# Per-head sums of squares: four tiles at a time in four column groups of TensorE, in place of one call for each tile

## The chip, the cores and the metric

The kernel runs on one core of one Trainium2 chip. The metric is the device time of one execution in microseconds. Three executions of the kernel before took 913.89, 914.31 and 915.83 us; the median, 914.31 us, is what the changed kernel is compared with.

## What is computed

Two transformer blocks over 512 tokens of width 1024, in f32. The first has gated mixing, a forgetting attention and a convolved feed-forward layer. The second, in which the change lies, has four heads of a gated delta rule (heads of 128) and four heads of a differential attention (each with two halves of 64). The parts that matter:

```python
# delta rule: q and k from a causal convolution with silu, heads of 128
q = l2norm(q) * 128 ** -0.5         # x * rsqrt(sum(x * x) + EPS)
k = l2norm(k)
# differential attention: 4 heads, 2 halves of 64 each
q = rmsnorm(q.reshape(b, t, 4, 2, 64), q_gain) * 64 ** -0.5
k = rmsnorm(k.reshape(b, t, 4, 2, 64), k_gain)
s = einsum('bqhcd,bkhcd->bhcqk', q, k)       # causal softmax over k
wts = p[:, :, 0] - lam * p[:, :, 1]
```

Each norm needs, for each token and head (or half head), a sum of squares over the head's channels.

## The kernel before

Activations are kept with channels on the partitions and tokens along the free dimension: a tile is 128 channels x 512 tokens. Large products are made in three f32r passes (a high and a low half of each operand, `three`, line 662), one weight tile of 128 x 1024 ("unit") at a time, from a ring of four slots that SP and POOL fill by DMA and whose low halves VectorE (DVE) makes (`ring_low`).

The second block follows one list, MIX2_ORDER (lines 339 to 353), that all engines walk in the same order. Each engine acts on the items that concern it, strictly in that order, and semaphores tie them together. The stages, in order:

- `_projections`: `kqv` 0 to 11 are the products of the delta rule's k (0 to 3), q (4 to 7) and v (8 to 11). `taps` is the convolution on DVE, then a silu on ScalarE (ACT) and, for q, a square into SQ2. The k norms come from elsewhere (the diagonal of the Gram matrices). `l2s` (line 1144, `head_sums` 924) sums the squares of one q tile: `token_sums` (723) makes four matmuls, in each of which 128 tokens of the squares are the stationary operand and a column of ones moves, so that the sums come out with tokens on the partitions. `l2r` (2093) copies them to L2C.
- `_diff_values`: `dfv` is the product of the attention's values, into banks 0, 6, 7, 1; between its parts run the decays, the Gram products and the start of the inverse.
- QUERIES_KEYS (line 143): `dfqk` (n, part) is an eighth of the product of tile n, q and k by turns. Tile n - 1 is squared by ACT at part 0 (1485) and summed at part 5 (`qk_sums`, 932), the last one at item (8, 1), with two moving columns for the two halves of a head, into bank 6. `qr` (1486) takes the root on ACT and the reciprocal on DVE (2105) for four tiles. `rs` or `kn` (1490) spreads a key's factors over RS on ACT; `kn` transposes RS into bank 7 (`spread_key`, 938) and DVE multiplies the key tile by it (2025). These items are mixed by `_prepare` and `_spread` (103, 262) with the steps of two block inverses (Y, Z, X, W), as their fills.
- `_attention(4)` (176) makes slots 0 to 18. Slot n holds D of n - 1, A of n and B of n - 2, and in every fourth from 6 on C. A: scores on PE (`df_scores`, 1076), masked maximum on DVE (`masked_max`, 2029), exponentials on ACT (1538). D: the difference of the two weightings, on DVE (2039). B: transposes on PE (`df_turn`, 1088) and a copy to PT2 on ACT (1548), which the next B on PE waits for. C: `df_attend` (1098). Between them stand eighths of the last projection, `z`. `_last_norms` (116) puts the last sums, `qr` 1, `rs` 2, `kn` 2, `rs` 3 and `kn` 3 into the first slots.

The first block has products in two column groups of the array already: `attend` (823) writes partitions 0 to 63 and 64 to 127 of a bank from two heads, with widths of 512, 384, 256 and 128 columns. `rows_to_columns` (917) transposes 128 x 512 in four steps.

## Time and profile before

| what | value |
|---|---|
| median of three runs | 914.31 us (913.89 to 915.83) |
| profiled execution, span from the first to the last instruction | 911.8 us |
| PE, matmuls | 896.3 us busy, 4467 records |
| PE, weight loads | 725.4 us |
| DVE | 556.8 us, 980 instructions |
| ACT | 291.4 us, 594 instructions |
| granted clock of PE over the span | 1.000 |

The page gives no other time of the profiled execution than its span. A busy time is the union of an engine's spans. Matmuls are pipelined: the durations shown overlap, so what a group of matmuls costs is read from starts, not from durations. An f32 matmul appears as two records, each with a weight load of its own; an f32r matmul or a transpose as one. Times in rows are microseconds from the span's start unless marked ns; "idle before <- releaser" is the time an engine stood idle ahead of an instruction and what released it.

### The profile page before, as it was taken

The numbers are of one execution on the slowest core, as the hardware profiler recorded it, in microseconds if no ns is written. First come the engines' busy times: TensorE is split into PE (matmuls) and PEld (weight loads), VectorE is DVE, ScalarE is ACT, GpSimd is POOL, SyncE is SP. The second block draws the span as 40 slices with busy tenths as digits, with TensorE's granted clock in tenths as the row PEclk, the third lists the DMA queues.
The fourth block names the chain that finished last, engine by engine and source line by source line (L and its number), as shares of the span: only waits on it lengthen the run. The fifth ranks groups of instructions, "written<-read, shape, count | busy, mean of one in ns | idle before, by whom it ended". The sixth has DMA issues, their size and how long they took to land.

```text
span 911.8 us, 13208 instructions
## 1 busy us (share of the span) xinstructions
PE 896.3 (98%) x4467; PEld 725.4 (80%) x4467; DVE 556.8 (61%) x980; ACT 291.4 (32%) x594; POOL 72.4 (8%) x138
## 2 busy tenths in 40 slices
PE   9999998999999999999999999999999999999998
PEld 7887766688888888888888888888888897567887
DVE  7248467355877777767743334497787473875555
ACT  6234466524322222222210101353231113444710
POOL 0000000000010110000100000000000000000000
PEclk9999999999999999999999999999999999999999
DMA  8856443254765566655566655568556222221554
GB/s 276 245 192 195 152 139 116 93 162 133 236 203 189 184 193 194 202 193 184 189 195 196 196 192 185 184 211 252 173 151 183 73 92 93 93 82 59 181 174 153
DMA packets 53861, 154.74 MB, mean 170 GB/s; under 512 B 9629, under 2 KB 15021, under 8 KB 53689
## 3 DMA queue, kind: packets, MB, share of 16 engines
q1 hardware_dynamic: 22320, 75.70, 26.0%
q0 software_dynamic: 19008, 69.21, 23.4%
q10 hardware_dynamic: 12488, 9.23, 3.3%
q8 instruction: 29, 0.48, 0.2%
q14 instruction: 16, 0.12, 0.0%
HBM read 149.63 MB, written 4.49 MB: 169 GB/s over the span
## 4 chain that ended last, share of the span: by engine, by line
PE 88%; DVE 5%; issue 3%; DMA 3%; ACT 2%; DVEq 0%; SPq 0%; POOLq 0%; ACTq 0%
PE bank L668 75%; DMA HI<-wstream 2%; PE bank L727 1%; PE bank L1104 1%; PE bank L805 1%; PE bank L1084 1%; DVE LO L1634 1%; PE bank L829 1%; PE bank L1015 1%; PE bank L1001 1%; PE bank L819 1%; PE bank L1095 1%; DMA RAW<-wstream 1%; DVE SQ L1616 0%; PE bank L1037 0%
## 5 line engine op out<-in xcount | busy, mean ns | idle before, releaser
L668 PE MATMUL bank<-GH,HI 128*128 128x512 f32 (+1 forms) x724 | 292.7, 404 | 1.1 <-issue 1.1
L668 PE MATMUL bank<-GH,LO 128*128 128x512 f32 (+1 forms) x724 | 281.8, 389 | 0.0
L668 PE MATMUL bank<-GL,HI 128*128 128x512 f32 (+1 forms) x724 | 281.4, 389 | 0.0
L1634 DVE TENSOR_TENSOR LO<-RAW,HI 128x1024 fp32r<-128x1024 f32 x88 | 107.6, 1223 | 119.3 <-DMA HI<-wstream 118.4
L668 PEld LDWEIGHTS bank<-GH,HI 128*128 128x128 f32 x724 | 136.1, 188 | 35.9 <-issue 9.8
L668 PEld LDWEIGHTS bank<-GH,LO 128*128 128x128 f32 x724 | 135.9, 188 | 28.8
L668 PEld LDWEIGHTS bank<-GL,HI 128*128 128x128 f32 x724 | 136.3, 188 | 23.4
L650 POOL DMA_DIRECT2D HI<-wstream x132 | 69.8, 529 | 815.3 <-PE bank L668 805.4
L1346 ACT ACTIVATE YC<-AB,PAR 128x512 f32<-128x512 f32 x44 | 36.0, 818 | 140.7 <-DVE AB L1798 140.7
L668 PE MATMUL bank<-AH,HI 128*128 128x512 f32 x176 | 69.4, 394 | 0.0
L668 PE MATMUL bank<-AH,LO 128*128 128x512 f32 x176 | 69.0, 392 | 0.0
L668 PE MATMUL bank<-AL,HI 128*128 128x512 f32 x176 | 68.3, 388 | 0.0
L1798 DVE TENSOR_TENSOR AB<-bank,RB 128x512 f32<-128x512 f32 x44 | 30.4, 691 | 48.9 <-PE bank L668 48.8
L1792 DVE TENSOR_TENSOR LO<-RAW,HI 128x1024 fp32r<-128x1024 f32 x44 | 53.6, 1218 | 3.2 <-DMA HI<-wstream 3.2
L668 PEld LDWEIGHTS bank<-AH,LO 128*128 128x128 f32 x176 | 33.0, 188 | 7.7
L1225 ACT ACTIVATE GH<-X,SM 128x512 fp32r<-128x512 f32 x8 | 5.8, 724 | 104.4 <-DVE X L1856 104.4
L668 PEld LDWEIGHTS bank<-AL,HI 128*128 128x128 f32 x176 | 33.0, 188 | 7.4
L668 PE MATMUL bank<-HI,GH 128*128 128x512 f32 x96 | 38.2, 398 | 0.5 <-DVE LO L1641 0.5
L668 PEld LDWEIGHTS bank<-AH,HI 128*128 128x128 f32 x176 | 33.1, 188 | 6.6
L668 PE MATMUL bank<-LO,GH 128*128 128x512 f32 x96 | 37.4, 390 | 0.0
L668 PE MATMUL bank<-HI,GL 128*128 128x512 f32 x96 | 37.4, 389 | 0.0
L1809 DVE SCALAR_TENSOR_TENSOR YC<-AB,PAR,YC 128x512 f32<-128x512 f32 x44 | 33.1, 751 | 6.0 <-DVE YC L1805 0.3
(309 smaller groups left out, 1173.3 us busy)
## 6 DMA issues: line engine op xcount, KB each, us to landing
RAW<-wstream SPq DMA_DIRECT2D x135, 512.0 KB, 3.7
HI<-wstream POOLq DMA_DIRECT2D x132, 512.0 KB, 5.0
X<-x_t SPq DMA_DIRECT2D x8, 256.0 KB, 7.6
NCB<-out_t ACTq DMA_DIRECT2D x8, 256.0 KB, 4.2
out_t<-X ACTq DMA_DIRECT2D x8, 256.0 KB, 5.5
XR<-out_t ACTq DMA_DIRECT2D x8, 256.0 KB, 3.5
out_t<-XR SPq DMA_DIRECT2D x7, 256.0 KB, 3.6
EG<-out_t ACTq DMA_DIRECT2D x1, 1024.0 KB, 6.1
```

Source lines behind the costliest of these rows:

```text
L650: pool.dma_start(HI[:, s, :], wstream[bass.ds(2 * i + s // 2, 1), :, 1024 * (s % 2):1024 * (s % 2 + 1)] .rearrange("o p n -> p (o n)")).th ...
L668: mm = pe.matmul(out, a, b, start=(first and n == 0), stop=(last and n == 2))
L727: mm = pe.matmul(out[:, n * b:n * (b + 1)], src[:, P * b:P * (b + 1)], groups, start=True, stop=True)
L805: mm = pe.matmul(PS[2 + e][:, 0:w], q[r, 4 + p, P * i:P * (i + 1)], k[r, p, 0:w], start=(part == 0), stop=(part == 2))
L819: mm = pe.transpose(PS[4 + e][:, P * j:P * (j + 1)], P1[:, 2 * (n % 2) + e, P * j:P * (j + 1)], IDENT)
L829: mm = pe.matmul(PS[6][64 * e:64 * e + 64, P * j:T], VB[:, j, P * p + 64 * e:P * p + 64 * (e + 1)], PT1[:, e, j, P * j:T], start=(j == 0), ...
L1001: mm = pe.matmul(narrow(A, h, l), NT[:, h, b, :], even(XI[:, h, b, :], l), start=True, stop=True)
L1346: act.activation(YC[:, gv, :], AB[:, gv, 2:T + 2], ACT.Identity, scale=PAR[:, bass.ds(6 * t + (C_FCW + 3 * gv + 2), 1)], bias=PAR[:, bass. ...
L1634: dve.tensor_tensor(LO[:, u % RING, :], RAW[:, u % RING, :], HI[:, u % RING, :].bitcast(F32), ALU.subtract).then_inc(unit_split, 1)
L1792: dve.tensor_tensor(LO[:, slot, :], RAW[:, slot, :], HI[:, slot, :].bitcast(F32), ALU.subtract).then_inc(unit_split, 1)
L1798: dve.tensor_tensor(AB[:, gv, 2:T + 2], up_bank(G_UP + 2 * tt + gv)[:, :], RB[:, :], ALU.mult)\
L1809: dve.scalar_tensor_tensor(YC[:, gv, :], AB[:, gv, 0:T], PAR[:, bass.ds(6 * t + (C_FCW + 3 * gv), 1)], YC[:, gv, :], ALU.mult, ALU.add).th ...
```

## The change

The sums are made for four tiles in one call, `four_sums`. Matmul j has 32 columns as its stationary operand (ones, or the indicators of the two half heads, 16 columns each) and all 512 tokens of tile j's squares as the moving one, and writes partitions 32j to 32j + 31 of bank 7, so that each uses one group of 32 columns of the array. The bank now holds rows with tokens along the free dimension. ACT copies it to SBUF (`l2c`, `qc`), and PE transposes the copy back into bank 7 (`turned_rows`; `l2t`, `qt`), from where `l2r` and `qr` read one column of each 32 or 16. SQ2 and SQD grow from two tiles to four. The items are moved: the sums of the delta rule's q stand behind `kqv` 9, their transposes behind `kqv` 10 and `l2r` behind the taps of tile 10. The first four of the attention's q and k are summed at (4, 5). In attention `qc` 1 stands ahead of A0, `qt` 1 behind A0, `qr` 1 behind A1, `rs` 2 and `kn` 2 in slots 2 and 3, `rs` 3 and `kn` 3 in slot 4. There are new waits: `dfv` waits for `l2r`, C of head 0 for all keys.

```diff
--- before.py
+++ after.py
@@ -115,10 +115,11 @@
 
 def _last_norms(slots):
 
-    slots[0] = [("z", (0, 0)), ("P", 0), QUERIES_KEYS[-1], ("qr", 1), ("rs", 2)] + slots[0]
-    slots[1] += [("P", 1), ("kn", 2)]
-    slots[2].insert(0, ("rs", 3))
-    slots[3] += [("P", 2), ("kn", 3)]
+    slots[0] = [("z", (0, 0)), ("P", 0), QUERIES_KEYS[-1], ("qc", 1)] + slots[0]
+    slots[1] = [("qt", 1)] + slots[1] + [("P", 1), ("qr", 1)]
+    slots[2] += [("rs", 2)]
+    slots[3] += [("P", 2), ("kn", 2)]
+    slots[4] = [("rs", 3)] + slots[4] + [("kn", 3)]
     return slots
 
 
@@ -146,7 +147,11 @@
     for n in range(9):
         for part in range(KC if n < 8 else 2):
             order.append(("dfqk", (n, part)))
-            if (n, part) == (5, 0):
+            if (n, part) == (4, 5):
+                order.append(("qc", 0))
+            elif (n, part) == (4, 7):
+                order.append(("qt", 0))
+            elif (n, part) == (5, 0):
                 order.append(("qr", 0))
             elif (n, part) in ((5, 4), (6, 0)):
                 order.append(("kn", n - 5))
@@ -274,8 +279,8 @@
 
     order = [("ba", 0), ("rows", 0)]
     for t in range(12):
-        if t in (6, 10):
-            order.append(("l2r", t // 4 - 1))
+        if t in (6, 11):
+            order.append(("l2r", t // 8))
         order.append(("kqv", t))
         if t == 0:
             order += [("lam", 0), ("rows", 1)]
@@ -287,8 +292,10 @@
             order.append(("cols", 0))
         if 4 <= t <= 7:
             order.append(("spill", t - 4))
-        if 6 <= t <= 9:
-            order.append(("l2s", t - 2))
+        if t == 9:
+            order += [("l2s", 0), ("l2c", 0)]
+        if t == 10:
+            order.append(("l2t", 0))
         if t == 7:
             order.append(("bt", 0))
         if t == 9:
@@ -340,8 +347,8 @@
     _projections()
     + _diff_values()
     + QUERIES_KEYS[:8] + [("T2", 1)] + QUERIES_KEYS[8:10] + [("scatter", 1)] + QUERIES_KEYS[10:21] + [("X", (0, 3)), ("X", (1, 3))] + QUERIES_KEYS[21:24]
-    + _prepare(0, QUERIES_KEYS[24:43])
-    + _prepare(2, QUERIES_KEYS[43:-1])
+    + _prepare(0, QUERIES_KEYS[24:45])
+    + _prepare(2, QUERIES_KEYS[45:-1])
     + _with_products(_last_norms(_attention(4)), _eighths(range(5))[1:36], [])
     + _merge(_eighths(range(4, 6))[4:13],
              _merge(_scans(range(3)), [("os", t) for t in range(4)] + [("or", 0)] + [("on", t) for t in range(4)]))
@@ -438,7 +445,7 @@
         R1 = place("R1", [P, T], F32, TR + 5 * KB)
         R2 = place("R2", [P, T], F32, TR + 7 * KB)
         BR = place("BR", [P, T], F32, TR + 11 * KB)
-        SQ2 = place("SQ2", [P, 2, T], F32, TR + 13 * KB)
+        SQ2 = place("SQ2", [P, 4, T], F32, TR + 13 * KB)
         ZT = place("ZT", [P, 8, T], F32, TR)
         SQO = place("SQO", [P, 2, T], F32, TR + 16 * KB)
         DQ = place("DQ", [P, 4, T], F32, arena + 72 * KB)
@@ -447,7 +454,7 @@
         RS = place("RS", [P, T], F32, arena + 96 * KB)
         ST = place("ST", [P, 4, P], F32, arena + 98 * KB)
 
-        SQD = place("SQD", [P, 2, T], F32, X_AT)
+        SQD = place("SQD", [P, 4, T], F32, X_AT)
         P0 = place("P0", [P, 3, T], F32, X_AT)
         PB = place("PB", [P, T], F32, X_AT + 6 * KB)
         PT2 = place("PT2", [P, NB, T], F32, X_AT + 8 * KB)
@@ -482,6 +489,7 @@
         IDENT, ONES, HALF = (CON[:, c:c + P] for c in (K_ID, K_ONE, K_HALF))
         CAUSAL = CON[:, K_CAUSAL:K_CAUSAL + 512]
         GNEG = CON[:, K_GNEG:K_GNEG + P]
+        ONES32, HALF32 = CON[:, K_ONE:K_ONE + 32], CON[:, K_HALF + 48:K_HALF + 80]
 
         def level_mask(l):
             n = MASKED.index(l)
@@ -725,6 +733,18 @@
                 n = groups.shape[1]
                 for b in range(NB):
                     mm = pe.matmul(out[:, n * b:n * (b + 1)], src[:, P * b:P * (b + 1)], groups, start=True, stop=True)
+                return mm
+
+            def four_sums(out, tiles, groups):
+
+                for j in range(4):
+                    mm = pe.matmul(out[32 * j:32 * j + 32, :], groups, tiles[:, j, :], start=True, stop=True)
+                return mm
+
+            def turned_rows(out, rows):
+
+                for b in range(NB):
+                    mm = pe.transpose(out[:, P * b:P * (b + 1)], rows[:, P * b:P * (b + 1)], IDENT)
                 return mm
 
             def over_rows(out, column):
@@ -921,19 +941,29 @@
                     mm = pe.transpose(PS[4][:, P * b:P * (b + 1)], RS[:, P * b:P * (b + 1)], IDENT)
                 mm.then_inc(rates_mm, 1)
 
-            def head_sums(t):
-                pe.wait_ge(l2_sq, t - 3)
-                token_sums(PS[7][:, NB * t:NB * (t + 1)], SQ2[:, t % 2, :]).then_inc(l2_mm, 1)
+            def head_sums():
+                pe.wait_ge(l2_sq, 4)
+                four_sums(PS[7], SQ2, ONES32).then_inc(l2_mm, 1)
+
+            def head_sums_turned():
+                pe.wait_ge(l2_rt, 1)
+                turned_rows(PS[7], SQ2[:, 0, :]).then_inc(l2_mm, 1)
 
             def rates_to_rows():
                 pe.wait_ge(beta_made, 1)
                 pe.transpose(PS[3][0:16, 0:P], BRK2.rearrange("p h b -> p (h b)"), IDENT).then_inc(rates_mm, 1)
 
-            def qk_sums(n):
-                pe.wait_ge(qn_sq, n + 1)
-                if n == 0:
+            def qk_sums(g):
+                pe.wait_ge(qn_sq, 4 * g + 4)
+                if g == 0:
                     pe.wait_ge(tiles_freed, FREED_DFV + 4)
-                token_sums(PS[6][:, 8 * n:8 * (n + 1)], SQD[:, n % 2, :], HALF[:, 0:P:HD]).then_inc(qn_mm, 1)
+                else:
+                    pe.wait_ge(qn_made, 2)
+                four_sums(PS[7], SQD, HALF32).then_inc(qn_mm, 1)
+
+            def qk_sums_turned(g):
+                pe.wait_ge(qn_rt, 2 * g + 1)
+                turned_rows(PS[7], RS).then_inc(qn_mm, 1)
 
             def spread_key(h):
                 pe.wait_ge(qn_sp, h + 1)
@@ -1099,6 +1129,8 @@
                 pe.wait_ge(dpt_freed, NB * (h + 1))
                 if h >= 1:
                     pe.wait_ge(dpv_freed, h)
+                else:
+                    pe.wait_ge(qn_made, 4)
                 for i in range(NB):
                     for j in range(i + 1):
                         mm = pe.matmul(PS[7][:, blk(i)], PT2[:, j, blk(i)], DV[:, j, blk(h)], start=(j == 0), stop=(j == i))
@@ -1140,9 +1172,14 @@
                         pe.wait_ge(gemm_freed, G_DFQK - 1)
                         pe.wait_ge(rb_ready, 3)
                         pe.wait_ge(r1_kept, 1)
+                        pe.wait_ge(l2_rc, 1)
                     product_tokens(U_DFV, DFV_BANKS, 2 * KC, (n,), (gemm_freed, G_DFQK))
                 elif what == "l2s":
-                    head_sums(n)
+                    head_sums()
+                elif what == "l2t":
+                    head_sums_turned()
+                elif what == "qt":
+                    qk_sums_turned(n)
                 elif what == "bt" and n == 0:
                     rates_to_rows()
                 elif what == "dfqk":
@@ -1151,8 +1188,8 @@
                         if n < 2:
                             pe.wait_ge(tiles_freed, FREED_DFV + (1, NB)[n])
                         product(U_DFQK + n, G_DFQK + n, gl_made, 2 * KC, ks=(part,))
-                    if n >= 1 and part == (5 if n < 8 else 1):
-                        qk_sums(n - 1)
+                    if (n, part) in ((4, 5), (8, 1)):
+                        qk_sums(n // 4 - 1)
                 elif what == "kn":
                     spread_key(n)
                 elif what == "GK":
@@ -1421,9 +1458,10 @@
                     act.activation(tile_of(n), tile_of(n), ACT.Silu).then_inc(cv_s, 1)
                     if 4 <= n < 8:
                         act.wait_ge(cv_s, n + 1)
-                        if n >= 6:
-                            act.wait_ge(l2_mm, n - 5)
-                        act.activation(SQ2[:, n % 2, :], tile_of(n), ACT.Square).then_inc(l2_sq, 1)
+                        act.activation(SQ2[:, n - 4, :], tile_of(n), ACT.Square).then_inc(l2_sq, 1)
+                elif what == "l2c":
+                    act.wait_ge(l2_mm, 1)
+                    act.activation(SQ2[:, 0, :], PS[7][:, :], ACT.Copy).then_inc(l2_rt, 1)
                 elif what == "egb":
                     act.wait_ge(scratch_stored, STORED_ROWS)
                     act.dma_start(EG[:, :, :], out_t[0:4, :].unsqueeze(0).to_broadcast([P, 4, T]))\
@@ -1480,13 +1518,19 @@
                         act.wait_ge(gemm_freed, G_DFQK + m + 1)
                         if m == 0:
                             act.wait_ge(x_spilled, 16 * (KC - 1))
-                        elif m >= 2:
-                            act.wait_ge(qn_mm, m - 1)
-                        act.activation(SQD[:, m % 2, :], tile, ACT.Square).then_inc(qn_sq, 1)
+                        elif m >= 4:
+                            act.wait_ge(qn_mm, 1)
+                        act.activation(SQD[:, m % 4, :], tile, ACT.Square).then_inc(qn_sq, 1)
+                elif what == "qc":
+                    act.wait_ge(qn_mm, 2 * n + 1)
+                    if n:
+                        act.wait_ge(qn_bc, 2)
+                    act.activation(RS[:, :], PS[7][:, :], ACT.Copy).then_inc(qn_rt, 1)
                 elif what == "qr":
-                    act.wait_ge(qn_mm, 4 * n + 4)
-                    act.activation(QKC[:, 32 * n:32 * (n + 1)], PS[6][:, 32 * n:32 * (n + 1)], ACT.Sqrt,
-                                   bias=EPSC[:, 2:3]).then_inc(qn_rt, 1)
+                    act.wait_ge(qn_mm, 2 * n + 2)
+                    act.activation(QKC[:, 32 * n:32 * (n + 1)].rearrange("p (j b e) -> p j b e", j=4, b=NB),
+                                   PS[7][:, :].rearrange("p (b j e c) -> p j b e c", b=NB, j=4, e=2)[:, :, :, :, 0],
+                                   ACT.Sqrt, bias=EPSC[:, 2:3]).then_inc(qn_rt, 1)
                 elif what == "rs" or (what == "kn" and n < 2):
                     act.wait_ge(qn_rc, n // 2 + 1)
                     if n:
@@ -2091,11 +2135,12 @@
                 elif what == "k2":
                     key_squares(n)
                 elif what == "l2r":
-                    dve.wait_ge(l2_mm, 4)
-                    dve.tensor_scalar(L2C[:, 4:8, :], PS[7][:, 16:32].rearrange("p (t b) -> p t b", b=NB),
+                    dve.wait_ge(l2_mm, 2)
+                    dve.tensor_scalar(L2C[:, 4:8, :],
+                                      PS[7][:, :].rearrange("p (b t c) -> p t b c", b=NB, t=4)[:, :, :, 0],
                                       P * P * EPS, P * P * EPS * EPS, ALU.mult, ALU.add).then_inc(l2_rc, 1)
                 elif what == "rk":
-                    dve.wait_ge(l2_rt, 1)
+                    dve.wait_ge(l2_rt, 2)
                     then(dve.tensor_tensor(COLS[:, :, 1, :], COLS[:, :, 1, :],
                                            L2C[:, 0:4, :].rearrange("p h b -> p b h"), ALU.mult))
                 elif what == "dfqk":
@@ -2103,7 +2148,7 @@
                     if n < 8 and part == KC - 1:
                         evacuate(G_DFQK + n, U_DFQK + n, (DQ if n % 2 == 0 else DK)[:, n // 2, :])
                 elif what == "qr":
-                    dve.wait_ge(qn_rt, n + 1)
+                    dve.wait_ge(qn_rt, 2 * n + 2)
                     dve.reciprocal(QKC[:, 32 * n:32 * (n + 1)], QKC[:, 32 * n:32 * (n + 1)]).then_inc(qn_rc, 1)
                 elif what == "kn":
                     normalise_key(n)
```

## Rows read from the trace of the kernel before

**Rows 1.** The page's first part: busy us, share of the span, instructions.
```profile
PE 896.3 (98%) x4467; PEld 725.4 (80%) x4467; DVE 556.8 (61%) x980; ACT 291.4 (32%) x594; POOL 72.4 (8%) x138
```

**Rows 2.** Busy time by stretches: ahead of attention, and its start.
```profile
654.00:769.00 115.00, 115.00 (x731) 98.62 (x730) 72.17 (x185) 24.77 (x39) 6.35 (x12) 1.00 0.39 117
772.00:800.00 28.00, 26.57 (x139) 16.55 (x138) 21.29 (x69) 14.15 (x45) 1.05 (x2) 1.00 0.29 92
```

**Rows 3.** The line of `token_sums`: count, ns min/median/max, first and last start.
```profile
L727 PE MATMUL bank<-CON,SQD x64: 165/251/272, 694.4 to 771.0; 128*128 128x2 f32 x64
...
L727 PE MATMUL bank<-CON,SQ x56: 165/250/271, 29.3 to 642.9; 128*128 128x1 f32 x56
```

**Rows 4.** PE in order of time around the last `head_sums`: start, us, line.
```profile
641.94 0.39 PE L668 MATMUL bank<-GH,LO 128*128 128x512 f32 x1
642.17 0.95 PE L727 MATMUL bank<-CON,SQ 128*128 128x1 f32 x8
...
643.30 0.39 PE L668 MATMUL bank<-GL,HI 128*128 128x512 f32 x1
```

**Rows 5.** The same around the first `attend`.
```profile
109.20 0.40 PE L668 MATMUL bank<-GH,LO 128*128 128x512 f32 x1
109.53 2.38 PE L829 MATMUL bank<-PT,VB 128*64 128x512 f32 x16
111.83 0.50 PE L668 MATMUL bank<-GH,HI 128*128 128x512 f32 x1
112.17 0.39 PE L668 MATMUL bank<-GL,HI 128*128 128x512 f32 x1
```

**Rows 6.** The weight loads of that `attend`.
```profile
110.01 0.14 PEld L829 LDWEIGHTS bank<-PT,VB 128*64 128x64 f32 x2 [0.29 <-issue]
110.44 0.14 PEld L829 LDWEIGHTS bank<-PT,VB 128*64 128x64 f32 x2 [0.29 <-issue]
```

**Rows 7.** PE around `rows_to_columns`.
```profile
616.93 0.39 PE L668 MATMUL bank<-GH,LO 128*128 128x512 f32 x1
617.16 0.60 PE L921 MATMUL bank<-CON,RS 128*128 128x128 f32 x4
...
617.83 0.40 PE L668 MATMUL bank<-GL,HI 128*128 128x512 f32 x1
```

**Rows 8.** ACT at the silu of tile 9; DVE at the evacuation of tile 11.
```profile
646.59 0.63 ACT L1421 ACTIVATE VT<-VT 128x512 f32<-128x512 f32 x1 [2.77 <-DVE VT L2077]
...
654.15 0.69 DVE L1626 TENSOR_TENSOR CB<-bank,RB 128x512 f32<-128x512 f32 x1 [1.25 <-PE bank L668]
```

**Rows 9.** ACT: table loads, the second root, the exponentials of A2.
```profile
673.79 1.28 ACT L1442 ACT_TABLE_LOAD   x1 [5.26 <-issue]
...
771.26 0.29 ACT L1488 ACTIVATE SM<-bank,SM 128x32 f32<-128x32 f32 x1 [1.14 <-PE bank L727]
...
772.61 1.28 ACT L1538 ACT_TABLE_LOAD   x1
...
779.80 0.58 ACT L1538 ACTIVATE P<-bank,SM 128x384 f32<-128x384 f32 x1 [1.08 <-DVE SM L2036]
```

**Rows 10.** DVE: the second reciprocal, `kn` 2, starts of D1 and D4.
```profile
771.58 0.35 DVE L2107 RECIPROCAL SM<-SM 128x32 f32<-128x32 f32 x1 [0.87 <-ACT SM L1488]
...
777.41 0.74 DVE L2027 SCALAR_TENSOR_TENSOR DK<-DK,PAR,bank 128x512 f32<-128x512 f32 x1
778.23 0.16 DVE L2046 RECIPROCAL SM<-SM 128x1 f32<-128x1 f32 x1
...
788.11 0.16 DVE L2046 RECIPROCAL SM<-SM 128x1 f32<-128x1 f32 x1
```

**Rows 11.** PE: the transposes of B1, B2 and B4.
```profile
781.35 0.41 PE L1095 MATMUL bank<-CON,P 128*128 128x128 f32 x2 [0.85 <-ACT PT L1548]
...
785.50 0.52 PE L1095 MATMUL bank<-CON,P 128*128 128x128 f32 x3 [0.59 <-ACT PT L1548]
...
791.11 0.27 PE L1095 MATMUL bank<-CON,P 128*128 128x128 f32 x1
```

## Prediction, made before the changed kernel was run

> **What bounds the kernel now.** The page's first part comes first: TensorE (PE) is busy for 98% of the span, VectorE (DVE) for 61% and ScalarE (ACT) for 32% [rows 1]. So I asked whether PE waits in the stages that the change touches. The table by stretches answers: from 654 to 769 us, which holds seven of the eight query/key sums, PE is busy for all 115.00 us, and its clock is granted in full; from 772 to 800 us, where attention starts, it is busy for 26.57 of 28 [rows 2]. In the first stretch every PE instruction taken out comes off the end. In the second PE is partly held by a chain through the other two engines, and work moved there must be followed through that chain.
>
> The sums to be replaced are the line of `token_sums`: 64 matmul records for eight query/key tiles, and of the 56 under SQ, 32 are those of the four query tiles (the other 24 are the three row norms, which stay) [rows 3]. One call of four matmuls is eight records: each f32 matmul runs as two passes, each with a weight load of 128 columns for a moving operand of one or two columns. What an insertion costs is read from starts, since ends overlap. From the last product pass before it (641.94) to the second one behind it (643.30) are 1.36 us; two ordinary steps of 0.23 (641.94 to 642.17) would be 0.46. The insertion costs **0.90 us** [rows 4].
>
> **What is removed.** Twelve such insertions, four for the query norms, eight for q and k of the differential attention: 12 x 0.90 = 10.8 us.
>
> **What is added on PE.** Three times `four_sums` and three times `turned_rows`.
>
> `turned_rows` is the four transposes that `rows_to_columns` already makes, x4 records in one pass each: 616.93 to 617.83, less 0.46, is **0.44 us** [rows 7].
>
> `four_sums` streams 512 f32 columns in two passes, in four column groups. The nearest row is `attend` of the first block, which uses two column groups: 16 records from 109.20 to 112.17 [rows 5]. In it a pass of 512 columns takes 110.44 - 110.01 = 0.43 us, and weight loads come in twos: both groups start together [rows 6]. Its passes are 2 x (512+384+256+128) columns for each group, at 0.43/512 us 2.15 us if the groups run side by side, 4.3 if not; it costs 2.97 - 0.46 = 2.51. So they run side by side, and entering the column mode, exposed weights and leaving cost 0.36. If four groups do as two do, `four_sums` is 2 x 0.43 + 0.36 = **1.21 us** (rounded down for its smaller weights). That is the low end. The high end is one group after another: 8 x 0.43 + 0.36 = 3.8 us. I take the low end, since the only column-tiled row has full overlap; that four f32 streams are twice what any row here reads is the doubt.
>
> The Trainium skill, "TensorE: Matmul & The Clock Gate", section "Measured speedup vs the span model", gives 3.07x for four row tiles at 512 columns, not 4x. By that factor the passes would be an estimated 0.26 us longer for each `four_sums`, and the forecast 0.8 us higher. No run here shows four tiles at once.
>
> **The other engines, up to the last sums.** Two PSUM-to-SBUF copies on ACT are added outside attention. The one in the projections stands before a silu ahead of which ACT is idle for 2.77 us, and an activation of this size takes 0.63 [rows 8]; the other (g = 0) has two product parts and three steps of the inverse between `four_sums` and `turned_rows`, over 3 us of PE work against about 1.3 us for the last pass, the copy and its semaphore. `l2r` is now behind the taps of tile 10, and DVE is idle for 1.25 us ahead of the evacuation of tile 11, which covers its 16 columns; so the new wait of `dfv` for it should be met [rows 8]. If not, it costs PE a few tenths. The squares wait less than before. The new slices spread the fills of the first inverse differently by one place; every step keeps over 0.8 us of PE work before its successor. All this I cost at nothing; its cover is the idle time of ACT and DVE. No DMA is added, and the DMA issues in ACT's queue behind the copies (beta, the last spill) are late by 0.6 us at most in work that nobody waits for then. SP's and POOL's queues are fed by PE's progress, and start earlier with it.
>
> So up to the last square, PE is ahead by 11 x 0.90 - 2 x (1.21 + 0.44) = 9.9 - 3.3 = **6.6 us**.
>
> **The start of attention.** Here I walk the new order with old times, as though the last square ended where it did. Before, ACT took a square root (771.26), loaded the Exp table (772.61, 1.28 us) and kept it; the Sqrt table had been loaded at 673.79 [rows 9]. Now `qr 1` stands behind the exponentials of A0 and A1. So ACT loads Exp, Sqrt and Exp again: **two more loads of 1.28**.
> - The last passes of `four_sums` end near 771.2, the copy by 771.9, and the Exp load by 773.2, 0.7 ahead of the old one. A0, D0 and A1 are 0.7 early; A1's exponentials end near 777.5.
> - Then Sqrt load 1.28, root 0.29, reciprocal 0.35 [rows 9, 10]: 779.4. DVE, which is in order, does D1 only then; it did it at 778.23 [rows 10]. The chain is **1.2 us late**. The second Exp load lies beside D1 and the maxima. A2's exponentials start at 781.0 for 779.80, the copy of B0 ends by 782.4, and PE's B1, which was already waiting for that copy at 781.35, goes at 782.5 [rows 9, 11].
> - In slot 4 `kn 3` puts its 0.74 us on DVE ahead of D4 (788.11) [rows 10]; it used to run in a gap of slot 3. The chain is then 1.9 us late, and PE's B4, 791.11, comes at 792.9 [rows 11]. Behind it stands C0, 20 records of PE work, and PE leads again.
>
> PE is **1.8 us late** by that point. This holds the 0.3 us by which the last `four_sums` exceeds an old call and the 0.44 of its transposes; they lie in time that PE would wait anyway. Bounds: nothing but these 0.75 us if DVE and ACT find slack that I don't see; 3.5 us if the two loads (2.57) and `kn 3` come whole on top of the 0.3.
>
> **Sum.** 6.6 - 1.8 = 4.8 us. The profiled execution has a span of 911.8 us (the page shows no other time of it); the median of the runs, 914.31, is 2.5 above it. The change touches nothing outside the span: 914.3 - 4.8 = **909.5**.
>
> **Rivals.**
> 1. *Two column groups at a time*, because four f32 streams of moving data don't come at full rate. For: no row shows more than two. Each `four_sums` costs 0.85 more: 6.6 - 1.7 - 1.8 - 0.85 = 2.2 us gained, 912.1. Chance 0.14.
> 2. *The attention chain loses more*, 3.5 us: 3.1 gained, 911.2. Chance 0.10.
> 3. *The chain absorbs the loads*: 5.8 gained, 908.5. PE's stalls in slots 2 to 4 [rows 11] speak against it. Chance 0.07.
> 4. *Staircase*: the two passes of a call follow in program order, and only the second overlaps the next group's first: five steps, 5 x 0.43 + 0.36 = 2.5 us. Then 9.9 - 5.9 - 1.8 - 1.3 = 0.9 gained, 913.4. `attend` would show three steps for each pair and shows two [rows 6]. This is the case in which the change doesn't do what it says. Chance 0.05.
> 5. *Slower: one group after another*, at 3.8 us: 9.9 - 8.5 = 1.4, less 1.8, less 2.6 for the last one: 3.0 lost, 917.3. The change loses from 9.9 - 2(x + 0.44) = 1.8 + (x - 1.21), x = 2.8 us for each `four_sums`. Against it stands the overlap of two [rows 5, 6]. Chance 0.06.
>
> **Numbers.** The forecast has a chance of 0.58. The range holds it, rivals 1 to 3, and a few tenths of disagreement between runs: 908.0 to 912.4; left out are 4 and 5 and the edges. A measurement of this kernel tells about 0.2%, 1.8 us. Faster by more takes the forecast and rivals 1 to 3, 0.89, less 0.03 because rival 1 lies close to the bound: 0.86. The same: 0.08. Slower: 0.06.
>
> **What would show it.** Right: four weight loads of 32 columns starting together, twice, and 1.2 us by starts for each insertion; 0.44 for each set of transposes; 115 of 115 us still busy ahead of attention; three table loads between A0 and A2 and B1's wait longer by about 1.2 us. Wrong: `four_sums` passes that start one by one or take longer than 0.43; a wait of PE at `dfv` or at `turned_rows`; attention's stalls unchanged, or grown by over 2 us.

## The result, and the profile after

The changed kernel takes **918.20 us** (median of 14 runs, 910.17 to 922.30), the one before 914.14 in the same sessions (14 runs, 912.30 to 915.84): ratio **1.0033 [1.0018, 1.0049]** (the medians alone give 1.0044), slower by 0.3 to 0.4%. The forecast was 909.5 in a range of 908.0 to 912.4, so even the sign was wrong. The profiled execution took 916.39 us, span 914.7. Two executions far off all others, one of run 0 (1794 us) and one of the kernel before beside runs 7 and 8 (3146 us), are left out of the ratios below.

Two things stand out before any view is opened. The runs spread over 12 us, those of before over 3.5; and the time goes with the mean granted clock, though not exactly: 910.17 us at 1.000, 910.44 at 0.996, 916.39 and 919.91 at 0.993, 919.0 to 922.3 at 0.991 and below. The kernel before had 1.000 in its profile, this one 0.993.

The work did shrink. The page's first part (as [rows 1]) has 60 matmul records fewer and 1.6 us less busy PE, ACT has five more instructions:

```profile
PE 894.7 (98%) x4407; PEld 720.0 (79%) x4407; DVE 556.3 (61%) x980; ACT 295.8 (32%) x599; POOL 72.4 (8%) x138
```

The time is in the stage that [rows 2] show as 115.00 of 115.00. The stretches of after (us, busy us and instructions of PE, PEld, DVE, ACT, POOL, then granted clock, DMA share, GB/s):

```profile
654.00:699.00 45.00, 45.00 (x240) 38.55 (x239) 37.37 (x107) 11.59 (x16) 3.18 (x6) 1.00 0.55 163
...
699.00:702.20 3.20, 1.03 (x5) 0.53 (x3) 0.00 (x0) 0.42 (x1) 0.53 (x1) 1.00 0.87 222
702.20:709.00 6.80, 6.11 (x22) 5.56 (x23) 3.88 (x12) 0.63 (x1) 0.00 (x0) 0.50 0.55 171
709.00:721.60 12.60, 12.60 (x84) 11.08 (x82) 7.50 (x17) 1.80 (x3) 0.53 (x1) 1.00 0.19 60
```

```profile
699.64 0.39 PE L676 MATMUL bank<-GH,LO 128*128 128x512 f32 x1
702.89 1.94 PE L1031 MATMUL bank<-XI,NT 128*128 128x64 f32 x8 [2.86 <-DMA XI<-out_t]
704.59 0.77 PE L676 MATMUL bank<-GH,HI 128*128 128x512 f32 x1
705.16 0.63 PE L676 MATMUL bank<-GL,HI 128*128 128x512 f32 x1
705.59 0.63 PE L676 MATMUL bank<-GH,LO 128*128 128x512 f32 x1
```

L1031 is `Y(0,4)`, the first product that PE makes in the assembly of the first block inverse (levels 4, 5 and 6, from sub-blocks that are inverted already). Its left factor XI is written to DRAM by one DMA and gathered back by eight from ACT's queue; the last of it lands (is there to be read) at 702.8. Behind the wait the product passes start 0.43 us apart (705.16 to 705.59) where 0.23 is usual. Over the same items of the order, `Y(0,4)` to `Y(0,6)`, 18.73 us pass here, 15.76 where the clock holds (first experiment): **the half clock costs 3.0 us, the wait 2.9**.

The same items can be compared by their starts in the two traces, this one less the one before: up to the products just ahead of XI's transfers the change had gained 1.81 us (from +0.52 at 581 us to -1.29 at 688); at `Y(0,6)` it is 2.63 us behind; the last sums come 0.40 late, the first late step of attention (B1) 1.53, and the end 2.9.

The new operations themselves cost what the forecast said:

```profile
639.86 0.39 PE L676 MATMUL bank<-GH,LO 128*128 128x512 f32 x1
640.18 1.06 PE L741 MATMUL bank<-SQ,CON 128*32 128x512 f32 x8
641.17 0.50 PE L676 MATMUL bank<-GH,HI 128*128 128x512 f32 x1
641.51 0.39 PE L676 MATMUL bank<-GL,HI 128*128 128x512 f32 x1
...
646.52 0.39 PE L676 MATMUL bank<-GH,LO 128*128 128x512 f32 x1
646.75 0.60 PE L747 MATMUL bank<-CON,SQ 128*128 128x128 f32 x4
...
647.42 0.39 PE L676 MATMUL bank<-GL,HI 128*128 128x512 f32 x1
```

`four_sums`: 639.86 to 641.51 is 1.65, less two steps of 0.23: **1.20 us** (forecast 1.21). `turned_rows`: 646.52 to 647.42, less 0.46: 0.44 (0.44).

### The profile page after: what moved, and what is told of

The parts are those of the page before. It is cut to its first block, busy times and chain, and to the rows that moved or that the text cites. A ratio compares the mean times of both kernels' runs of the same rounds, so it can differ in the third digit from the quotient of the medians.

```text
span 914.7 us, 13093 instructions
## 1 busy us (share of the span) xinstructions
PE 894.7 (98%) x4407; PEld 720.0 (79%) x4407; DVE 556.3 (61%) x980; ACT 295.8 (32%) x599; POOL 72.4 (8%) x138
## 4 chain that ended last, share of the span: by engine, by line
PE 88%; DVE 5%; DMA 3%; issue 2%; ACT 2%; ACTq 0%; SPq 0%; DVEq 0%; POOLq 0%
PE bank L676 76%; DMA HI<-wstream 1%; PE bank L849 1%; PE bank L825 1%; PE bank L1136 1%; PE bank L1114 1%; PE bank L839 1%; PE bank L1031 1%; PE bank L1045 1%; DMA RAW<-wstream 1%; DVE LO L1678 1%; PE bank L1125 1%; DMA XI<-out_t 0%; DMA out_t<-XS 0%; PE bank L1102 0%
```

## Experiments

The account to be tested: the loss is the wait at `Y(0,4)` and the fall of the clock behind it, both because PE's order now reaches `Y(0,4)` before the XI transfers can be there. The rivals put it in one of the two parts of the change by itself, in attention, or in where the inverse starts; each expectation gives the numbers of its theories. The projection part is the four query tiles of the delta rule (`head_sums`), the query/key part the eight others. The runs have the numbers of their labels. Each ratio is to runs of the kernel before from the same session: their medians were 914.30 us (runs 1 to 4), 913.81 (5, 6, 0), 914.47 (7, 8) and 914.53 (9, 10).

### 1. The wait filled with idle products

```diff
                 elif what == "Y":
+                    if n == (0, 4):
+                        for _ in range(12):
+                            pe.matmul(PS[7][:, :], GH[:, 0, 0:P], GH[:, 0, :], start=True, stop=True)
                     inverse_y(*n)
```

> The changed kernel with 12 matmuls of 128x512 f32r into the free bank 7 put on TensorE just ahead of the first step of the inverse, Y(0,4); they are 12 x 0.23 = 2.7 us of work whose result nobody uses. Theory A (TensorE reaches Y(0,4) before the sub-block inverses have landed from HBM, waits 2.9 us there, and the granted clock falls to 0.5 for 6.8 us behind that wait, which costs another 3.7 us): the added work lies in the wait, the wait falls to under 0.5 us, the clock stays at 1.0 between 690 and 770 us, and the time is 3 to 4 us below the changed kernel's, near 914.5. Theory B (the time goes to the new order of steps in the inverse and in attention, and the wait is incidental): TensorE has 2.7 us more to do, and the time is the same as the changed kernel's or up to 2.7 us above it.

**912.29 us** (11 runs, 911.26 to 914.20), ratio 0.9980 [0.9972, 0.9989]. With 2.7 us of useless work added, the kernel is 5.9 us faster than the change by the medians. That is more than theory A's 3 to 4: the two profiled executions differ by 4.7 (916.39 and 911.66), and most other runs of the change are slower than its profiled one. Its stretches beside those of after:

```profile
699.00:702.20 3.20, 3.20 (x16) 2.65 (x15) 0.39 (x1) 0.21 (x1) 0.53 (x1) 1.00 0.88 265
702.20:709.00 6.80, 6.80 (x50) 6.24 (x48) 6.20 (x16) 0.63 (x1) 0.00 (x0) 1.00 0.50 148
```

and the fill and `Y(0,4)` in PE's order of time:

```profile
699.63 2.88 PE L1204 MATMUL bank<-GH 128*128 128x512 f32 x12
702.35 1.00 PE L1031 MATMUL bank<-XI,NT 128*128 128x64 f32 x8
703.15 0.48 PE L676 MATMUL bank<-GH,HI 128*128 128x512 f32 x1
703.47 0.39 PE L676 MATMUL bank<-GL,HI 128*128 128x512 f32 x1
```

The fill, 2.72 us by starts, takes the place of the wait of 2.86 (`Y(0,4)` comes at 702.35 in place of 702.89), so it saves 0.5 us of the wait at most; what it saves is the half clock, 50 instructions against 22 in the same 6.8 us. By starts that is 3.0 us, where the expectation had 3.7. In all 11 runs the mean clock is 0.996 or above; the change had that in 4 of 14. That the fall of the clock at `Y(0,4)` comes from the idle PE is shown here.

### 2. The inverse started later

```diff
-    ... QUERIES_KEYS[10:21] + [("X", (0, 3)), ("X", (1, 3))] + QUERIES_KEYS[21:24]
-    + _prepare(0, QUERIES_KEYS[24:45])
-    + _prepare(2, QUERIES_KEYS[45:-1])
+    ... QUERIES_KEYS[10:25] + [("X", (0, 3)), ("X", (1, 3))] + QUERIES_KEYS[25:28]
+    + _prepare(0, QUERIES_KEYS[28:48])
+    + _prepare(2, QUERIES_KEYS[48:-1])
```

> The changed kernel with the start of the first inverse, from the transposes X(0,3) and X(1,3) and from Y(0,4) on, four eighths of a query/key product later (4 x 0.69 = 2.8 us); no work is added or taken out. Theory A: the wait at Y(0,4) all but goes, the clock holds there, and the time falls by 2.9 + 3.7 = 6.6 us against the changed kernel, to 911 to 912; the longer wait in attention stays. Theory B: the steps of the inverse then have fewer products between them and the attention is unchanged: no gain against the changed kernel, or a loss of 1 to 2 us by waits of TensorE between the steps of the inverse.

**918.68 us** (6 runs, 918.13 to 921.98), ratio 1.0056 [1.0042, 1.0070]: a miss, no better than the change. The wait at `Y(0,4)` is gone, but I had moved the split between the two `_prepare` calls too, and with it the fills of the stage behind. Now PE waits at `kn 1`, and the clock falls there:

```profile
738.00:740.20 2.20, 0.94 (x9) 0.95 (x10) 1.57 (x4) 1.15 (x2) 0.00 (x0) 1.00 0.95 285
740.20:747.10 6.90, 6.90 (x29) 6.32 (x28) 4.48 (x12) 0.00 (x0) 0.00 (x0) 0.51 0.13 45
```
```profile
739.25 0.66 PE L973 MATMUL bank<-CON,RS 128*128 128x128 f32 x4 [2.29 <-ACT RS L1539]
```

A wait of 2.3 us in another place, for another engine, brings the same 6.9 us of half clock. A start moved alone was still to be tried (run 5). The same edit on the kernel before (run 0):

> The kernel before, without the change, with the start of the first inverse four eighths later. A control: TensorE has no wait at Y(0,4) there, so the later start has nothing to remove. Theory A: no gain, 914.3 within 0.5 us, or slower where kn 1 waits. Theory B (the later start is a gain by itself and explains what the changed kernel gains by it): 2 us or more below the kernel before.

915.86 us, ratio 1.0021 [1.0005, 1.0036]. It waits 1.4 us at `kn 1` as well, so it compares nothing cleanly.

### 3 and 4. Each part of the change alone

Run 3 is the kernel before with only `head_sums` in the new form; run 4 has only `qk_sums` in it, with the orders that belong to it.

> The part of the change in the projections alone (sums of the delta rule's four query tiles); the differential attention's sums as before. It takes 4 x 0.90 - 1.20 - 0.44 = 2.0 us off TensorE ahead of Y(0,4). Theory A: before the change TensorE came to Y(0,4) 0.9 us after the landing, so 0.9 us of the 2.0 is kept and 1.1 us becomes a wait there; the wait is too short to cost the clock: 913.0 to 913.5, the same or barely faster. Theory B: the projections are not where it is lost, and all of it shows: 912.2.

**912.41 us** (12 runs, 910.72 to 916.39), ratio 0.9978 [0.9966, 0.9991]: 1.9 us gained. My account had expected 1.1 us of this gain to be swallowed at `Y(0,4)`; none is, and there is no wait:

```profile
700.83 0.89 PE L1021 MATMUL bank<-XI,NT 128*128 128x64 f32 x7
```

These four calls stand ahead of the whole XI chain, so the chain's start moved with PE (issue 693.58, landing 699.91). PE still reaches `Y(0,4)` 0.9 us behind the landing, as before the change. Only time taken out *between* the chain's start and its consumer comes back as a wait.

> The part of the change in the differential attention's queries and keys alone. Ahead of Y(0,4) the two calls for tiles 0 and 1 are gone, 1.8 us. Theory A: 0.9 us of that becomes a wait at Y(0,4), the clock holds there; behind it 0.2 + 2.7 us are gained, and 2.1 us are lost at the start of attention to the two table loads: 912.5 (1.6 us gained), 2 us more if the clock falls in attention. Theory B: the loss is in this part, so it is as slow as the whole change or slower: 918 or above.

914.78 us (12 runs, 910.56 to 923.89), ratio 1.0025 [0.9996, 1.0055]: the total can't be told from before, but the wait can:

```profile
PE bank L1025 <- DMA XI<-out_t: 2.4, 1, 2.4
```

So the wait belongs to the query/key part, whose calls for tiles 0 and 1 stood between; it is longer than the 0.9 us expected (more on this in run 10). In this profile the clock held through 2.4 us of waiting; the runs range from 910.56 us at a clock of 1.000 to 923.89 at 0.989. Whether it falls behind such a wait differs from execution to execution.

### 5. Only the start of the inverse moved

```diff
-    ... QUERIES_KEYS[10:21] + [("X", (0, 3)), ("X", (1, 3))] + QUERIES_KEYS[21:24]
-    + _prepare(0, QUERIES_KEYS[24:45])
+    ... QUERIES_KEYS[10:25] + [("X", (0, 3)), ("X", (1, 3))] + QUERIES_KEYS[25:28]
+    + _prepare(0, QUERIES_KEYS[28:45])
```

Four items of filler go from behind `X` to ahead of it; nothing behind `_prepare(0)` moves. `Y(0,4)` and `Y(1,4)` stand next to each other as a result.

> The changed kernel with the start of the first inverse four query/key eighths (2.8 us) later, as in the run before that moved it, but with the second inverse and the key spreads (kn) in the order of the changed kernel. That run had no wait at Y(0,4) and a new one of 2.3 us at kn 1, which its shifted list had put directly behind the product that kn 1's factors follow. Theory A (the change loses by TensorE reaching Y(0,4) ahead of the landing, and by the clock behind that wait): no wait at Y(0,4), none at kn 1, clock at 1.0 up to attention, and the 2.7 us of added work of the filled-stall run are now products that had to be done anyway: 912.3 - 2.7 = 909.6, between 909 and 911 with the clock in attention. Theory B (fewer products between the steps of the first inverse cost as much as the wait): waits of over 1 us in total between its steps, 912 or more.

**909.12 us** (6 runs, 908.26 to 910.74), ratio 0.9943 [0.9926, 0.9959]: 4.7 us below the median of before (5.2 by the ratio) and 9.1 below the change. PE is never idle there and the clock is whole:

```profile
699.00:709.00 10.00, 10.00 (x66) 9.03 (x65) 7.31 (x18) 0.63 (x1) 0.53 (x1) 1.00 0.57 180
```

The same start given to the kernel before (run 8):

> The kernel before with exactly the later start of the first inverse that the best version has (second inverse and kn in the order of the kernel before). Theory A: nothing to remove at Y(0,4), no new wait at kn 1: 914 within 0.7 us of the kernel before. Theory B (the later start is a gain by itself): 911 or less, and the change would then bring only what is left.

913.19 us (12 runs, 912.38 to 914.34), ratio 0.9989 [0.9979, 0.9999]: about a tenth of a per cent (0.2 at most by the interval; 1.3 us by the medians) comes from the place of the start itself; the rest is the new sums'.

### 6. The last four tiles in the old form

Run 5 with the last four tiles summed, rooted and normalised by the old calls in their old places.

> The run with the later start of the inverse, but the sums of the last four query/key tiles, their root and the key spreads in the form and the places of the kernel before (four separate calls into bank 6, root ahead of A0, one table load at the start of attention). It costs TensorE three more calls of 0.90 = 2.7 us ahead of attention and removes the two table loads between A0 and A2. Theory A (the loads and kn 3 make attention 2.1 us later): 2.7 - 2.1 = 0.6 us slower than the run with the later start where both hold the clock, and faster than it wherever the longer wait in attention costs the clock; TensorE's wait at B1 back from 1.9 to 1.1 us. Theory B (the loads lie beside other work, the longer wait has another cause): the wait at B1 stays at 1.9 us, and the time is 2.7 us above the run with the later start.

908.99 us (6 runs, 908.31 to 911.63), ratio 0.9941 [0.9923, 0.9959]. The medians tell no difference from run 5. In the traces the last late step (A7) is 2.55 us behind run 5's, of which 1.87 had arisen in block one, where the code is the same; 0.68 remain, beside the 0.6 expected, and B1's wait is 0.85 us against 1.91 in run 5. By these two traces, then, the new form is worth 0.7 us for the last four tiles: its saving, less what the longer chain through attention costs.

### 7 and 10. Half the fill, and time put back in its place

Run 7 is run 1 with 6 products in place of 12. Run 10 puts time back where the removed calls stood:

```diff
                         product(U_DFQK + n, G_DFQK + n, gl_made, 2 * KC, ks=(part,))
+                    if (n, part) in ((1, 5), (2, 5)):
+                        for _ in range(4):
+                            pe.matmul(PS[7][:, :], GH[:, 0, 0:P], GH[:, 0, :], start=True, stop=True)
```

> The changed kernel with 6 matmuls into the free bank ahead of Y(0,4) instead of 12: 1.4 us of work, so that about half of the wait is left. A dose of the same thing. Theory A (the wait is set by the landing, and beyond some length it costs the clock): Y(0,4) starts at the same time after the landing as in the changed kernel and in the filled one, the wait is 1.0 to 1.6 us, the mean clock of all runs is at 0.996 or above, and the median is at 912 to 913, as with twelve. Theory B (each added matmul costs its own time, and the gain of the twelve had another cause): the time is not near the one with twelve; it lies halfway between the changed kernel's 918 and 912.3, or above.

911.59 us (12 runs, 910.03 to 919.39), ratio 0.9971 [0.9951, 0.9990]. I expected a wait of 1.0 to 1.6 us to remain; its profile shows none at `Y(0,4)`. Here XI landed 5.97 us after its first issue, where after needed 8.2. Eleven of the runs have a mean clock of 0.996 or above, as expected; the twelfth, 919.39 us at 0.989, has not, and where its clock fell no trace says.

> The changed kernel with 4 matmuls of 0.23 us into the free bank at the places of each of the two calls that stood between the start of the substitution's transfers and Y(0,4), that is at (1, 5) and (2, 5): TensorE's time there is as before the change, and so is the moment at which it frees the weight slot. Theory A, with the part that is open: of the 2.9 us of wait 1.8 are these two calls, and the rest is that the eight small transfers of XI landed 8.2 us after their first issue where they took 6.6, while the next weight load was asked for 3.3 us behind that issue and not 4.6. If that collision delays them, they land after about 6.6 us here, there is no wait at Y(0,4), and the median is 912 to 913. If their time varies for another reason, they still take 7.5 us or more, and a wait of 0.5 to 1 us is left. Theory B (the new order of the steps): 918, no change.

911.59 us (9 runs, 910.39 to 913.34), ratio 0.9962 [0.9947, 0.9977], no wait at `Y(0,4)`. 1.8 us of empty work in the two places does away with a wait of 2.9. The transfers account for the rest. XI's issue (ACT's queue), the next request of weights (POOL's) and the landing (the start of the transpose that waits for it) in after:

```profile
694.57 4.18 ACTq L1504 DMA_DIRECT2D XI<-out_t  x8
...
697.89 0.54 POOL L658 DMA_DIRECT2D HI<-wstream  x1 [8.49 <-issue]
...
702.78 1.30 DVE L2041 STREAM_TRANSPOSE XT<-XI 128x512 f32<-128x512 f32 x2 [5.85 <-DMA XI<-out_t]
```

in this run:

```profile
694.34 3.84 ACTq L1507 DMA_DIRECT2D XI<-out_t  x8
...
698.55 0.54 POOL L658 DMA_DIRECT2D HI<-wstream  x1 [9.39 <-issue]
...
700.80 1.30 DVE L2044 STREAM_TRANSPOSE XT<-XI 128x512 f32<-128x512 f32 x2 [3.57 <-DMA XI<-out_t]
```

and in the kernel before:

```profile
695.49 3.84 ACTq L1466 DMA_DIRECT2D XI<-out_t  x8
...
700.12 0.54 POOL L650 DMA_DIRECT2D HI<-wstream  x1 [9.42 <-issue]
...
702.12 1.31 DVE L1997 STREAM_TRANSPOSE XT<-XI 128x512 f32<-128x512 f32 x2 [3.32 <-DMA XI<-out_t]
```

Where the weights were asked for 3.1 to 3.3 us after XI's first issue, XI took 7.4 to 8.2 us to land (after, runs 1, 2 and 4); where it was 3.5 to 4.6 us, 6.0 to 6.8 (before and runs 3, 5, 6, 7, 9 and 10; in 5, 6 and 9 nothing waited for the landing, and the figure is a bound from above). In the kernel POOL waits with this request for PE's `unit_done`, so a faster PE brings it nearer to the small transfers. That the two then get in each other's way is the likely reason and is not shown: these are eleven single profiled executions that agree, and no run changed the weight transfer alone.

### 9. The square root in an idle gap of ACT

```diff
 # on top of run 5, in _last_norms
-    slots[1] = [("qt", 1)] + slots[1] + [("P", 1), ("qr", 1)]
-    slots[2] += [("rs", 2)]
-    slots[3] += [("P", 2), ("kn", 2)]
-    slots[4] = [("rs", 3)] + slots[4] + [("kn", 3)]
+    slots[1] = [("qt", 1)] + slots[1][:1] + [("P", 1), ("qr", 1)] + slots[1][1:] + [("rs", 2)]
+    slots[2] += [("kn", 2), ("rs", 3)]
+    slots[3] += [("P", 2), ("kn", 3)]
```

> The run with the later start of the first inverse (909.1), and in attention the second root moved from behind A1 to ahead of it, behind the low half of the next weight unit, where ScalarE was idle for 2.5 us between the exponentials of A0 and A1; rs 2 stands behind A1, kn 2 and rs 3 at the end of slot 2, kn 3 in slot 3. Work and table loads stay the same. Theory A (attention is late by 2.0 us because the Sqrt load, root and reciprocal stand on the chain from A1 to D1, and kn 3 ahead of D4): both loads now lie mostly in that idle time, B1's wait falls from 1.9 to about 1.0 us, and 1 to 1.5 us more are gained: 907.6 to 908.1. Theory B (the lateness is from the loads wherever they stand, or from the order of the key spreads): B1's wait stays at 1.9 us and the time at 909.

**906.44 us** (6 runs, 905.50 to 909.10), ratio 0.9909 [0.9889, 0.9929]: the fastest version, 0.9% below before and 1.3% below the change; 2.7 us below run 5, where 1.0 to 1.5 were expected. The spans of the two profiles differ by 2.9: 0.4 of it had arisen in block one, where the code is the same, and 2.2 arise in attention up to A7. In after, the root stands behind the exponentials of A1, and both table loads lie between A1 and A2:

```profile
777.93 1.28 ACT L1531 ACT_TABLE_LOAD   x1
779.23 0.29 ACT L1531 ACTIVATE SM<-bank,SM 128x32 f32<-128x32 f32 x1
779.53 1.28 ACT L1582 ACT_TABLE_LOAD   x1
781.33 0.58 ACT L1582 ACTIVATE P<-bank,SM 128x384 f32<-128x384 f32 x1 [0.51 <-DVE SM L2080]
```

Now it stands ahead of A1, in the time in which ACT waited 2.47 us for DVE's maxima:

```profile
766.54 1.28 ACT L1530 ACT_TABLE_LOAD   x1
767.83 0.29 ACT L1530 ACTIVATE SM<-bank,SM 128x32 f32<-128x32 f32 x1
768.14 1.28 ACT L1581 ACT_TABLE_LOAD   x1
769.43 0.47 ACT L1581 ACTIVATE P<-bank,SM 128x256 f32<-128x256 f32 x1
```

B1's wait (1.9 us in after and in run 5) is gone, where 1.0 had been expected to stay; a wait of 0.63 us at `kn` 2 is new. The edit also moves `kn` 2, `rs` 3 and `kn` 3 forward, and no run parts that from the root's place. All in all PE idles less at the start of attention, run 5 first and then run 9:

```profile
762.00:792.00 30.00, 27.40 (x143) 16.36 (x141) 21.04 (x63) 16.86 (x45) 1.58 (x3) 1.00 0.33 105
```
```profile
760.00:790.00 30.00, 29.27 (x155) 18.18 (x154) 21.34 (x63) 18.26 (x49) 1.58 (x3) 1.00 0.33 105
```

## Why the prediction was wrong

**The step that failed** is the sentence on the first stretch, "every PE instruction taken out comes off the end", and with it "All this I cost at nothing". I took PE's 115.00 busy of 115.00 us [rows 2] to mean that no other limit was near. It only says that none had been reached. What the trace of before held is above: XI lands at 702.12, and PE's `Y(0,4)` starts at 703.04, with no idle time ahead of it, so the slack is **0.9 us**:

```profile
703.04 1.00 PE L1001 MATMUL bank<-XI,NT 128*128 128x64 f32 x8
```

The calls for tiles 0 and 1, 1.8 us, lie between the chain's start and `Y(0,4)`, and so 0.9 us of them had to come back as a wait, whatever else happened. The other 2.0 of the 2.9 come from XI itself: eight gathers that took 8.2 us instead of 6.6, and an issue 0.4 us later behind the store. I followed ACT's and DVE's queues past the new copies, and wrote that the DMA queues merely start earlier; I did not ask whom an earlier weight request would meet.

**The second size**, which no rival priced, is the clock. Behind the wait it is granted at half for 6.8 us, which costs 3.0.

The prediction's own sign of being right, PE busy for all 115 us ahead of attention, fails by these waits: 2.86 us idle from 699 to 721 and 0.61 from 721 to 769.

**The sum again.** The forecast for the profiled execution's span was 911.8 - 4.8 = 907.0 us; it was 914.7, 7.7 more: wait 2.9, half clock 3.0, a wait of 0.8 (by starts) at `kn 1`, 0.5 in block one, 0.2 less gained ahead of XI's transfers than forecast (1.81 for 1.96), 0.3 more lost in attention (2.1 for 1.8), 0.4 behind it. Together 8.0 by unrounded terms, 0.3 too much. The 0.5 arose in code that did not change. The clock stood at 0.5 there for 3.4 us, but profiles with a whole clock in block one leave it anywhere from 0.5 us earlier than before (run 4) to 1.6 later (run 2), so it is not shown to be the clock's. The wait at `kn 1` was costed at nothing too. It comes with the query/key part, not with the first wait: runs 1, 4, 7 and 10 show it (0.6 idle), before, run 3 and run 5 don't. Its row in after:

```profile
744.85 0.66 PE L973 MATMUL bank<-CON,RS 128*128 128x128 f32 x4 [0.61 <-ACT RS L1539]
```

The median is 1.8 us above this execution. Six of the fourteen runs have a lower clock than it (0.991 to 0.987) and take 919.0 to 922.3, which speaks for more such stretches than this profile holds; but one run of 919.91 has the same 0.993, so the clock alone doesn't explain the spread. Where the time lay in those runs, no trace says.

The measured 918.2 also lies near the 917.3 of rival 5. That is chance: its mechanism, one column group after another at 3.8 us a call, did not happen.

**What was right.**
- *The prices.* 1.20 and 0.44 us against 1.21 and 0.44. Four column groups of 512 f32 columns run together: the eight passes, two for each group, have a median of 604 ns each by the records, and the whole call spans 1.06 us. All eight weight loads start together (the forecast had four, twice). Rivals 1, 4 and 5, which doubted it, are out:

```profile
640.17 0.16 PEld L741 LDWEIGHTS bank<-SQ,CON 128*32 128x32 f32 x8 [0.35 <-issue]
...
L741 PE MATMUL bank<-SQ,CON x8: 592/604/617, 640.2 to 640.6; 128*32 128x512 f32 x8
```

  By the factor of 3.07 that the Trainium skill ("TensorE: Matmul & The Clock Gate", section "Measured speedup vs the span model") gives for four row tiles, the call would take an estimated 1.47 us. These are column tiles, and the trace decides: 1.20 us, no loss by that factor.
- *The walk through attention.* Chain late by 1.2 at B1: 1.13 measured (1.53 less the 0.40 by which the last sums came late). PE late by 1.8 behind it: 2.1 in after, 2.0 in run 5, both at A7. Rivals 2 (3.5) and 3 (0.75) are out. The table loads take 1.28 us each. It is also where run 9 found 2.7 us: I had walked through it without asking whether the root and the key spreads could stand elsewhere.
- *The sum with the wait out of the way.* Run 5 is the change with one start moved: 909.12 us for the forecast's 909.5, a gain of 4.7 for 4.8. At its last sums PE is 7.2 us ahead of before, 6.6 forecast. That it comes so near is in part luck: the later start by itself was worth 1.3 us (run 8, by the medians), and against run 8 the new sums gain 4.1.

**The sign.** The change does the work it says, 10.8 us out and 4.9 in (3 x 1.64), and loses on account of a wait in a stage that it hardly touches. The run of the change at a full clock, 910.17 us, shows what is left when the clock happens to hold; 10 of the 14 runs lie above the median of before.

**Open.** Why the clock falls behind a wait in one execution and not in another. It fell behind 2.9 us in after and held behind 2.4 in run 4's profile. Behind B1's wait, 1.9 us in each of them, it fell to 0.5 for 3.4 us in after, run 4 and run 10, and held in runs 1, 2, 5 and 7. The stretch in after:

```profile
784.20:787.50 3.30, 3.30 (x12) 2.14 (x10) 2.95 (x9) 2.24 (x6) 0.00 (x0) 0.50 0.00 0
```

Open too: why XI lands early in run 7 with the same code ahead of it as run 1; and what drops the clock in block one in some executions. The half clock in attention cost only 0.1 us in after: that stretch is bound by the chain through ACT and DVE (B1 to A7 is 13.88 us, and 13.74 in run 5 with a whole clock).

## What to carry to other kernels

A stage in which PE is busy for the whole span can still stand less than a microsecond behind the landing of a transfer. Before costing removed PE work as a gain, list the consumers of every DMA chain behind it, take the slack of each (start of the consumer less the landing), and subtract from it the work removed between the chain's start and the consumer. That gave 0.9 of the 2.9 us here; the transfers themselves, which took longer, gave the other 2.0, so leave a margin. Where the slack turns negative, move the chain's start by as much; moving the start by four eighths of a product was worth 9 us here. A wait can cost its own length again in clock (2.9 us of waiting, 3.0 of half clock); where it can't be removed, filling it with idle products was better here than waiting.

## What the runs showed of the hardware

- An idle stretch of PE of 2.9 us (after) or 2.3 us (run 2) was followed by a granted clock of 0.5 for 6.8 and 6.9 us; behind 2.4 us (run 4) it held. Behind 1.9 us at B1 it fell for 3.4 us in three profiles (after, runs 4 and 10) and held in four (runs 1, 2, 5 and 7). The price was 3.0 us where PE was the bound and 0.1 where it wasn't.
- Adding 2.7 us of empty products in place of a wait made a kernel 5.9 us faster (run 1, medians).
- Eight small gathers landed 7.4 to 8.2 us after their first issue where a weight load was asked for 3.1 to 3.3 us behind it, and 6.0 to 6.8 where it was 3.5 to 4.6: seen in eleven profiled executions, not isolated.
- Two f32 passes of 512 columns in four column groups cost 1.20 us with entering and leaving, as estimated from two groups (1.21).
